# Moving the weight rings, the parameters and one operand place to other SBUF addresses in a one-layer decoder step

## What is computed

```python
def _layer(x, mem_k, mem_v, pool_prev, conv_prev, pos0, norm_mix, w_in, w_pool, pool_scale,
           conv_w, w_out, norm_attn, w_q, w_o, norm_mlp, w_up, w_down):
    h = _rms(x, norm_mix)
    proj = h @ w_in                                   # 2048 -> 4096: u, B, C, v
    ...
    ya, new_pool = _pool_mixer(pool_prev, u, pos0, w_pool, pool_scale)
    yb, new_conv = _conv_mixer(conv_prev, bg, cg, v, conv_w)
    x = x + jnp.concatenate([ya, yb], axis=-1) @ w_out
    x = x + _cross_attn(_rms(x, norm_attn), mem_k, mem_v, w_q, w_o)   # 4 heads of 512, 256 memory tokens
    hm = _rms(x, norm_mlp) @ w_up                     # 2048 -> 8192
    x = x + jnp.square(jax.nn.relu(hm)) @ w_down      # 8192 -> 2048
    return x, new_pool, new_conv
```

## The kernel before

| tensor | before | mod 2,048 | mod 64 | after | mod 2,048 | mod 64 |
|---|---|---|---|---|---|---|
| inner_a, operand places 0 to 3 | 16512 + 17408n | 128 or 1152 | 0 | the same | | |
| residual, operand places 4 and 5, late | 120960 + 17408n | 128 or 1152 | 0 | the same | | |
| par | 204928 | 128 | 0 | 155776 | 128 | 0 |
| unit_raw | 155776 | 128 | 0 | 157696 | 0 | 0 |
| unit_high | 172160 | 128 | 0 | 174080 | 0 | 0 |
| unit_low | 188544 | 128 | 0 | 190464 | 0 | 0 |
| rstd, unit_sum | 206720 | 1920 | 0 | 206848 | 0 | 0 |
| temp_0, probs, heads_6 | 212128 | 1184 | 32 | 212256 | 1312 | 32 |
| operand place 6 (tokens_6, tokens_late_6, hidden_1_5) | 211936 | 992 | 32 | 211904 | 960 | 0 |
| its second half (hidden_1_6) | 220640 | 1504 | 32 | 220608 | 1472 | 0 |

## Time and profile before

### The profile page before, as it was taken

The page is one execution under the profiler, slowest core; times in us unless marked ns, Lnnn a source line. Parts: engine busy times, 40 slices in busy tenths (PEclk is TensorE's granted clock), DMA queues, the critical chain, the costliest instruction groups (busy, mean ns, idle before and its releaser), DMA issues.

```text
span 2531.1 us, 46810 instructions
## 1 busy us (share of the span) xinstructions
PE 2512.6 (99%) x19432; PEld 2445.2 (97%) x19432; DVE 2109.4 (83%) x2621; ACT 1201.2 (47%) x1683; POOL 181.1 (7%) x288
## 2 busy tenths in 40 slices
PE   9999999999999999999999999999999999999997
PEld 8889999999999979799999999999999999999997
DVE  8899888888686678679888888888888888888888
ACT  6455555444453353435655555555543333333344
POOL 1000000000000020000111110000000000000000
PEclk9999999999999999999999999999999999999999
DMA  8663433474434385542666666556686566656533
GB/s 297 217 217 121 149 110 127 151 273 145 140 131 160 124 318 189 214 144 85 221 221 223 220 222 210 199 194 210 221 311 213 191 223 213 210 186 216 203 126 104
DMA packets 139305, 483.74 MB, mean 191 GB/s; under 512 B 12800, under 2 KB 19072, under 8 KB 127840
## 3 DMA queue, kind: packets, MB, share of 16 engines
q1 hardware_dynamic: 95264, 265.07, 31.8%
q0 software_dynamic: 43424, 215.52, 23.1%
q10 hardware_dynamic: 416, 0.30, 0.0%
HBM read 387.45 MB, written 93.39 MB: 190 GB/s over the span
## 4 chain that ended last, share of the span: by engine, by line
PE 92%; DVE 5%; issue 2%; ACT 1%; DMA 0%; DVEq 0%; ACTq 0%; SPq 0%
PE psum_main L3480 29%; PE psum_side L3480 22%; PE psum_main L3120 11%; PE psum_side L3120 8%; PE psum_main L2992 7%; PE psum_main L3094 3%; PE psum_main L3034 2%; PE psum_main L3424 2%; PE psum_main L3195 1%; PE psum_main L3039 1%; PE psum_side L3195 1%; PE psum_main L3359 1%; PE psum_main L3294 1%; DVE unit_low L1940 1%; PE psum_side L3424 1%
## 5 line engine op out<-in xcount | busy, mean ns | idle before, releaser
L1608 ACT ACTIVATE unit_high<-unit_raw 128x1024 fp32r<-128x1024 f32 x382 | 398.7, 1056 | 521.3 <-PE psum_main L3480 146.1
L2629 DVE TENSOR_TENSOR unit_low<-unit_raw,unit_high 128x1024 fp32r<-128x1024 f32 x382 | 465.2, 1221 | 94.3 <-ACT unit_high L1608 94.1
L3480 PE MATMUL psum_main<-tokens_late,unit_high 128*128 128x272 f32 x2048 | 276.9, 287 | 0.1
L1940 DVE TENSOR_TENSOR unit_low<-unit_raw,unit_high 128x1024 fp32r<-128x1024 f32 x176 | 214.7, 1221 | 72.0 <-ACT unit_high L1206 71.6
L1206 ACT ACTIVATE unit_high<-unit_raw 128x1024 fp32r<-128x1024 f32 x176 | 185.0, 1057 | 187.5 <-DVE unit_raw L1963 45.6
L3480 PE MATMUL psum_main<-hidden,unit_high 128*128 128x272 f32 x1984 | 267.8, 287 | 0.0
L3480 PEld LDWEIGHTS psum_main<-tokens_late,unit_high 128*128 128x128 f32 x2048 | 264.1, 188 | 0.3 <-ACT tokens_late L1147 0.3
L3480 PEld LDWEIGHTS psum_main<-hidden,unit_high 128*128 128x128 f32 x1984 | 255.8, 188 | 0.0
L3120 PE MATMUL psum_main<-tokens,unit_high 128*128 128x272 f32 x1536 | 208.2, 288 | 0.2 <-DVE conv_lines L1991 0.2
L3480 PE MATMUL psum_side<-tokens_late,unit_high 128*128 128x272 f32 x1536 | 207.8, 287 | 0.3 <-DVE tokens_late L1848 0.3
L3480 PE MATMUL psum_side<-hidden,unit_high 128*128 128x272 f32 x1488 | 200.9, 287 | 0.0
(11 more groups left out here) (398 smaller groups left out, 4423.5 us busy)
## 6 DMA issues: line engine op xcount, KB each, us to landing
unit_raw<-weights SPq DMA_DIRECT2D x423, 512.0 KB, 4.5
hidden<-hidden_kept POOLq DMA_DIRECT2D x56, 1088.0 KB, 6.0
hidden_kept<-hidden_staged POOLq DMA_DIRECT2D x31, 1904.0 KB, 7.4
unit_sum<-weights SPq DMA_DIRECT2D x44, 512.0 KB, 3.6
residual<-x_t POOLq DMA_DIRECT2D x16, 544.0 KB, 6.6
residual_kept<-residual_new POOLq DMA_DIRECT2D x32, 272.0 KB, 2.3
cache_ring_q<-cache_k POOLq DMA_DIRECT2D x8, 1024.0 KB, 6.4
cache_ring_a<-cache_k POOLq DMA_DIRECT2D x8, 1024.0 KB, 6.2
```

What stands on the lines that cost most here:

```text
L1608: act.activation(WHI[:, slot, :], raw, ACT.Copy).then_inc(mlp_high, 1)
L1940: dve.tensor_tensor(shaped(q, WLO[:, slot, :]), block_in(q, source), shaped(q, WHI[:, slot, :]).bitcast(F32), ALU.subtract).then_inc(in_re ...
L2629: dve.tensor_tensor(WLO[:, slot, :], raw, WHI[:, slot, :].bitcast(F32), ALU.subtract) \
L3480: ins = pe.matmul(bank, w[:, slot, col:col + P], moving[:, k, part, :], start=start and k == 0 and n == 0, stop=k == kk - 1 and n == 2, sk ...
```

## The change

Three lines of addresses. The parameters go in front of the rings, with 128 more bytes of room than they need, so the rings begin at multiples of 2,048; a room of 256 bytes at the end becomes 128; the seventh operand place is rounded down to a multiple of 64 instead of 32.

```diff
@@ -260,10 +260,10 @@
         CACHE_Q = [at(f"cache_ring_q{n}", [P, GROUPS, 512], F32, x_at + (8 + 4 * n) * TOK * 4) for n in range(2)]
+        PAR = at("par", [P, PARAMS], F32, room(PARAMS * 4 + 128))
         RAW = at("unit_raw", [P, RING, UNIT], F32, room(RING * UNIT * 4))
         WHI = at("unit_high", [P, RING, UNIT], F32R, room(RING * UNIT * 4))
         WLO = at("unit_low", [P, RING, UNIT], F32R, room(RING * UNIT * 4))
-        PAR = at("par", [P, PARAMS], F32, room(PARAMS * 4))
@@ -278,7 +278,7 @@
-        room(256)
+        room(128)
@@ -309,7 +309,7 @@
-                              [place[0] // 32 * 32 - CH * 2 * HALF * 4] for other in (x_at, b_at))
+                              [(place[0] - CH * 2 * HALF * 4) // 64 * 64] for other in (x_at, b_at))
```

## The result

| | before | changed |
|---|---|---|
| median | 2533.69 us (2532.8 to 2534.22, 7 runs) | 2541.86 us (2541.06 to 2542.21, 7 runs) |
| span of the profiled execution | 2531.1 us | 2540.5 us |
| TensorE busy | 2512.6 us | 2521.8 us |

The change makes the kernel slower: ratio 1.0032, 95% interval 1.0023 to 1.0041, 8.2 us by the medians and 9.4 us between the two profiled executions. 2531.4 us had been forecast; 2541.9 lies above the range, on the side of rival B.

The account below looks back on a forecast made before the run. TensorE, busy 2512.6 of 2531.1 us, was taken as the bound. Savings of 1.1 + 0.5 = 1.6 us from 2532.89 gave 2531.3, plus 0.1 for the median: 2531.4 us, 8-in-10 range 2513 to 2537.5.

Parts of the forecast that it names:

- rival B: In the products, weight loads and streams meet in SBUF and delay the next matmul: 1.3 ns each, 2552 us; chance 0.13.
- TensorE's spacing is the only thing that can move: Whole kernel: no instruction or wait changes, so only matmul spacing and the length of work TensorE waits for can matter.
- part 3's zero: ScalarE, VectorE and ring loads at new addresses: helpers stay under cover, loads cost 0, with 0.7 us to either side.
- Part 1: Seventh operand place at a multiple of 64: w_up, mixing, queries and odd w_down chunks save 1.1 us, bounds 0 and 1.5.
- Part 2, the argument of the circle: Rings moved, 16,128 matmuls of the products: four k-tiles go round a 512-byte circle, so shifting weights by 128 changes 0.
- Part 2, the streams outside the products: Line 2992 and the key and value projections, with a constant address relation: gain 0.5 us together; bounds 2.0 and 1.8 us.
- Rival A: Ring-reading matmuls: weights tiles stop paying for straddling a boundary of 512, 0.66 ns each, 2519 us; chance 0.29.
- The estimate of 2364: All 18,750 ring-reading matmuls: if the rings' place alone kept them from 115.8 ns, some 167 us less, 2364 us.
- two independent read ports: TensorE reads weights and stream independently, so part 2 as a whole would be 0 and the time 2531.9 us.
- Its point of decision: In the products, rival B decides as soon as 0.31 ns a matmul is lost (5.1 us / 16,128).
- lines of 16 bytes: SBUF counted in lines of 16 bytes: part 1 would give 0 and the sum would lose 1.1 us.

Follow-up runs that it names:

- place_only: Only the seventh operand place rounded down to a multiple of 64, rings left in place, against the kernel before: 2533.71 us, ratio 0.9999.
- rings_only: The change without its rounding of the seventh operand place, so only parameters and rings move, against the kernel before: 2540.9 us, ratio 1.003.
- w160: 32 bytes of room ahead of the rings (160 past a multiple of 2,048), seventh place at a multiple of 64, against the kernel before: 2534.75 us, ratio 1.0005.
- after_turned: The changed kernel with all its addresses, MLP k-tiles taken in the order 1, 2, ..., 0: 2536.18 us, ratio 1.001 to the kernel before.
- before_turned: The kernel before with all its addresses, MLP k-tiles taken in the order 1, 2, ..., 0: 2537.69 us, ratio 1.0016.
- shift_all: Parameters in front of everything, so operands and rings move together, rings at multiples of 2,048, against the kernel before: 2534.04 us, ratio 1.0002.
- w320: 192 bytes of room ahead of the rings (320 past a multiple of 2,048), own_row moved into a gap, against the kernel before: 2553.05 us, ratio 1.0076.
- w160_mem32: Rings at 160 past a multiple of 2,048, the memory's split tiles also moved by 32 bytes, against the kernel before: 2531.57 us, ratio 0.9991.
- w384: Parameters in front of the rings without the 128 extra bytes, rings 384 past a multiple of 512, against the kernel before: 2532.99 us, ratio 0.9998.
- w256: 128 bytes of room ahead of the rings, which begin 256 past a multiple of 2,048, against the kernel before: 2542.72 us, ratio 1.0037.

## Why the prediction was wrong

- **TensorE's spacing is the only thing that can move.** Right. The busy row took nearly all of it; the costs of ScalarE, VectorE and the loads stayed where they were (the one load on the chain took 7.18 us for 6.99), and part 3's zero holds.
- **Part 1, 1.1 us less.** Beside rings left in place the size was about right (1.0 us by place_only's quads), but by luck: the reason was wrong, and beside the moved rings, as in the change itself, the same rounding costs 1.3 us (the change against rings_only). "32 past a multiple of 64 costs" was read from one address. w160's products pay nothing for it, and the same place 6 at a multiple of 64 takes 3.027 us in w_down's product 6. What differed was the distance from the tiles (modulo 256, 96 before and 64 in place_only) and what had run just ahead.
- **Part 2, the argument of the circle: this is the step that failed.** Its first half held and even fell short: the two addresses act on each other through their distance alone, modulo 256 and not 512. Its second half said "Shifting the weights by 128 turns that circle by one step and leaves its sum". Turning the circle costs 13.4 ns a product, because the time of a matmul depends on what ran ahead of it: begun at the other distance, the second pass falls into the rhythm of 120.8 and 132.5. after_turned and before_turned show exactly this step, one way and the other. A sum over a set of cases is only safe if no case depends on the one ahead; the trace had the warning in the earlier trace rows, where product 6, as far off 64 as product 5, was not as long. The prediction saw it, under rival B, and weighed it too lightly.
- **Part 2, the streams outside the products, 0.5 us less.** Line 2992 gained 0.8 us, the sign as forecast. The value projection lost 2.2 us and the key projection 0.5, where their bound had been 1.8 for both: 13.4 ns over the columns was taken for nearly the worst, and 19.0 was measured. Together these streams cost 1.9 us more instead of 0.5 less.
- **Rival A** (straddling a boundary) is refuted by shift_all. The estimate of 2364 from the Trainium skill's 115.8 ns (TensorE: Matmul & The Clock Gate, Back-to-back issue gap), whose formula that section gives for an isolated matmul and not for a stream of weight loads and matmuls, had no row behind it and gets none: no address tried brought the average of a product of 272 columns below 124.4 ns a matmul. The same page's two independent read ports for weights and stream (Step-by-step: what each phase is for) gave part 2 a zero; the runs disagree. From 2.993 to 3.027 us a product, 1.1%, hangs on the distance between the two operands and the order in which the distances come, so where the weights lie does change the time of the stream.
- **Rival B** named what happened, a sum that depends on where the circle begins. Its reason, reads that meet in the same part of SBUF, is not shown by any run. Its price, 1.3 ns a matmul, was too high for this distance: 0.56 ns was paid. Its point of decision, 0.31 ns, was passed. At the worst distance, w320's, 1.4 ns are paid.
- **The Trainium skill's lines of 16 bytes** (SBUF — State Buffer, Specifications) would have made every address of this case alike, since all are multiples of 32. The four spacings of the table do not fit that. w160's products alone would; its value projection does not.

## What to carry to other kernels

Where TensorE is back to back, where an operand lies is part of the kernel, but no address is good or bad by itself: look at the stream's start less the weights tile's start, modulo 256, and at the order in which a loop meets these values. That holds for what was run here, float32r matmuls that each load their own tile. Rounding everything to a large power of two can as well land on a bad relation; shifts of the rings in steps of 64 bytes moved this kernel by up to 0.76%, and turning the loop over k-tiles took back the MLP's share of such a loss without moving anything. Try the four shifts and read the spacing of 24 matmuls from the chain, which shows 13 ns in 3,000, where the intervals of the medians are 2 us and more to either side.

## What was not expected

- A spacing that has a memory over hundreds of matmuls. w160 and w160_mem32 have the same addresses in the MLP. In w160's profiled execution the first even chunk ran at 20.953 us a quad from its second quad on; in w160_mem32's it ran at 21.09 for the other three quads (the 6.03 rows above) and on into the first odd quad, some 620 matmuls with 3.013 us a product. Behind that quad's products 5 and 6, which are at other distances, it was back at 2.993. The products of the two kernels are the same instructions at the same addresses, so more than one spacing is possible for them; that costs or gives 0.14 us a quad. Each was seen in one profiled execution. What decides between them, and how often it happens, was not tried.
- For products that follow others at the same distance, with the rings at multiples of 64, the distance modulo 256 and the loop's order are enough to tell the spacing to the nanosecond: before, w384 and shift_all agree, and so do the change and w256. Where a product at another distance ran ahead they are not: at distance 64 a product takes 2.987 us behind one at distance 0, and 3.027 behind one at 64 (place_only's products 5 and 6 in the odd chunks), and at distance 0 one takes 2.993 or, behind one at 192, 3.018 (shift_all's product 0).
- What inside the chip makes the rhythms stays open. That reads of weights and of streams meet in parts of SBUF that repeat every 256 bytes would fit all runs, but none of them shows it.
